# VectorE's ranking halves placed around each dot, and TensorE's background products and queries in halves behind each row's sum

## What is computed

```python
def peer(x, w_q, sub_keys, u_tab, v_tab):
    q = (x @ w_q).reshape(B, S, PEER_HEADS, 2, PEER_HALF)
    scores = jnp.einsum('bshpk,hpnk->bshpn', q, sub_keys)
    s1, i1 = lax.top_k(scores[:, :, :, 0, :], PEER_TOPK)
    s2, i2 = lax.top_k(scores[:, :, :, 1, :], PEER_TOPK)
    cand = (s1[..., :, None] + s2[..., None, :]).reshape(B, S, PEER_HEADS, PEER_TOPK * PEER_TOPK)
    top_s, top_c = lax.top_k(cand, PEER_TOPK)
...
    gates = jax.nn.softmax(top_s, axis=-1).astype(x.dtype)
...
        ue = jnp.take(u_tab, idb, axis=0)
        h = jnp.einsum('thkd,td->thk', ue, xb)
        act = gb * jax.nn.gelu(h, approximate=False)
        ve = jnp.take(v_tab, idb, axis=0)
        return jnp.einsum('thk,thkd->td', act, ve)
```

## Time and profile before

| | |
|---|---|
| median of 3 runs | 1421.67 us (1417.94 to 1422.74) |
| the profiled execution | 1421.98 us, span 1420.3 us |
| mean granted clock of PE | 0.896 of full speed |
| PE, DVE, ACT, POOL busy | 80%, 76%, 66%, 44% of the span |
| read from HBM | 578.60 MB, 409 GB/s over the span |

### The profile page before, as it was taken

The page is one execution under the profiler, slowest core; times in us unless marked ns, Lnnn a source line. Parts: engine busy times, 40 slices in busy tenths (PEclk is TensorE's granted clock), DMA queues, the critical chain, the costliest instruction groups (busy, mean ns, idle before and its releaser), DMA issues.

```text
span 1420.3 us, 19525 instructions
## 1 busy us (share of the span) xinstructions
PE 1130.9 (80%) x6884; PEld 890.8 (63%) x6884; DVE 1078.1 (76%) x2602; ACT 938.8 (66%) x1617; POOL 625.0 (44%) x572
## 2 busy tenths in 40 slices
PE   9999999998789877696756987877667866776566
PEld 4567777676677776666656566765555655555455
DVE  1488877778778887678766668988887788878857
ACT  2245778679877988766645666667666766667563
POOL 1044444344444554444433434444444555444451
PEclk9999999999889999998777988898789988888968
DMA  9899999999999999999999999999999999999994
GB/s 351 311 383 409 422 425 425 426 425 425 402 426 419 424 423 425 425 424 417 431 422 425 426 426 406 426 425 426 426 426 413 404 423 426 426 425 426 425 400 170
DMA packets 94476, 581.98 MB, mean 410 GB/s; under 512 B 10237, under 2 KB 15781, under 8 KB 31914
## 3 DMA queue, kind: packets, MB, share of 16 engines
q0 software_dynamic: 79552, 536.91, 90.5%
q1 hardware_dynamic: 14826, 43.83, 8.0%
HBM read 578.60 MB, written 2.10 MB: 409 GB/s over the span
## 4 chain that ended last, share of the span: by engine, by line
DMA 40%; PE 30%; DVE 15%; ACT 8%; issue 6%; POOL 2%; SPq 0%; DVEq 0%; POOLq 0%; ACTq 0%
DMA arena<-in_uv,ids 39%; PE ps L1269 11%; DVE arena L1914 8%; ACT arena L1536 3%; PE ps L1082 3%; PE ps L948 3%; POOL arena L691 2%; PE ps L1159 2%; PE ps L740 2%; ACT actv L1529 1%; PE ps L757 1%; PE ps L896 1%; PE ps L824 1%; PE ps L821 1%; ACT L1576 1%
## 5 line engine op out<-in xcount | busy, mean ns | idle before, releaser
L691 POOL DMA_INDIRECT arena<-in_uv,ids x556 | 619.9, 1115 | 734.5 <-DVE hid L1914 338.0
L1269 PE MATMUL ps<-ident,arena 128*128 128x128 f32 x4076 | 608.9, 308 | 273.0 <-ACT arena L1536 271.2
L1269 PEld LDWEIGHTS ps<-ident,arena 128*128 128x128 f32 x4076 | 533.3, 159 | 364.6 <-ACT arena L1536 321.4
L1914 DVE CUSTOM_DVE_ANT_1 arena<-arena 128x1024 f32<-128x1024 f32 x384 | 467.7, 1224 | 187.2 <-DMA arena<-in_uv,ids 183.8
L1536 ACT ACTIVATE arena<-arena,actv 128x1024 f32<-128x1024 f32 x511 | 554.2, 1131 | 0.3 <-ACT actv L1529 0.2
L1526 ACT ACTIVATE gel<-hid 128x2 f32<-128x2 f32 (+1 forms) x257 | 52.0, 202 | 356.0 <-DVE hid L1914 353.2
L1914 DVE CUSTOM_DVE_ANT_0 arena<-arena 128x1024 f32<-128x1024 f32 x128 | 155.4, 1223 | 61.1 <-DMA arena<-in_uv,ids 58.5
L1529 ACT ACTIVATE actv<-gel,gates 128x1 f32<-128x1 f32 x511 | 122.9, 287 | 8.4
L948 PE MATMUL ps<-arena 128*128 128x128 f32 x992 | 120.3, 281 | 0.0
L948 PEld LDWEIGHTS ps<-arena 128*128 128x128 f32 x992 | 118.2, 199 | 0.0
L1082 PE MATMUL ps<-arena 128*128 128x384 f32 x192 | 65.9, 486 | 0.0
(11 more groups left out here) (269 smaller groups left out, 1018.1 us busy)
## 6 DMA issues: line engine op xcount, KB each, us to landing
arena<-in_wq SPq DMA_DIRECT2D x9, 1024.0 KB, 10.2
arena<-in_uv,ids POOLq DMA_INDIRECT x556, 3.8
arena<-in_w_out SPq DMA_DIRECT2D x2, 2048.0 KB, 11.3
arena<-in_w_gate SPq DMA_DIRECT2D x1, 4096.0 KB, 17.2
arena<-in_w_out SPq DMA_DIRECT2D x3, 1024.0 KB, 13.1
arena<-in_w_k SPq DMA_DIRECT2D x4, 512.0 KB, 7.9
arena<-in_w_q SPq DMA_DIRECT2D x2, 1024.0 KB, 10.2
arena<-in_w_v SPq DMA_DIRECT2D x2, 1024.0 KB, 10.2
```

What stands on the lines that cost most here:

```text
L691: nc.gpsimd.indirect_dma_start(out=dst, out_offset=None, in_=a["uv"][:, :], in_offset=bass.IndirectOffsetOnAxis(ap=ids[:, u % 4, c:c + 1], ...
L1269: i = mm(ps[:, run_bank(r) + k // 4, (k % 4) * P:(k % 4 + 1) * P], v_row(u, c)[:, k * P:(k + 1) * P], ident[:, :], is_transpose=True, star ...
L1914: v.tensor_tensor_reduce(out=r, in0=r, in1=x1[t], scale=1.0, scalar=0.0, op0=ALU.mult, op1=ALU.add, accum_out=hid[:, i, c:c + 1]).then_inc ...
```

## The change

On DVE each of the five parts of the ranking is split in two. Part 0 stands between the two dots of a group, part 1 behind the second. Unit 0 keeps its old order. The first MAX_INDEX of a key ranking gets a wait for its own end. On PE each product of four blocks is split into two of two blocks: the first behind the odd row of the step, the second behind the next even row. A query is split into its two halves of eight matmuls, one behind row 10 or 11, the other behind the row after. No computation is added or removed, and the order on POOL, ACT and SP is the same.

```diff
@@
-            def query(u):
+            def query(u, half):
                 t, h, b = UNITS[u]
-                pe.wait_ge(wq_in[b], 16 * len(wq_homes[b]) * wq_load(u)[1])
-                pe.wait_ge(score_used, EARLY[u][0] + 2 if u in EARLY else u)
...
+                if half == 0:
+                    pe.wait_ge(wq_in[b], 16 * len(wq_homes[b]) * wq_load(u)[1])
+                    pe.wait_ge(score_used, EARLY[u][0] + 2 if u in EARLY else u)
...
+                if half == 1:
+                    i.then_inc(q_done, 1)
@@
-            def piece_half(p, half):
+            def piece_half(p, half, part):
                 kind, b = PIECES[p]
-                if half == 0 and p >= 2:
+                k0 = 4 * half + 2 * part
+                if k0 == 0 and p >= 2:
                     wait_taken(p - 2)
@@
+            def products(step, part):
+
                 for p in range(NP):
                     for half in range(2):
                         if step == HALF_AT[p][half]:
-                            piece_half(p, half)
+                            piece_half(p, half, part)
+                for t in range(1, NT):
+                    for i in range(1, 5):
+                        if step == out_step(t, f"p{i}"):
+                            out_product(t, i, part)
+                for i in range(NT - 1):
+                    b = TAIL_AT[TAILS[i]]
+                    if step == b + 1 and i == 0 and part == 0:
+                        pe.wait_ge(bias_kept, 2)
+                    if step in (b + 1, b + 2):
+                        k = 4 * (step - b - 1) + 2 * part
+                        gate_product(i, 0, HALF, k, k + 2, 6)
+                    if step in (b + GATE_1, b + GATE_1 + 1):
+                        k = 4 * (step - b - GATE_1) + 2 * part
+                        gate_product(i, HALF, D, k, k + 2, 4)
@@
             for u in range(NU):
                 for c in range(TOPK):
                     combine(u, c)
+                    if c % 2 == 0 and u * TOPK + c:
+                        products((u * TOPK + c) // 2 - 1, 1)
...
-                    if c == query_row(u) and u + 2 < NU and u + 2 not in EARLY:
-                        query(u + 2)
-                    for e in kept_early(u, c):
-                        query(e)
+                    for half in range(2):
+                        if c == query_row(u) + half and u + 2 < NU and u + 2 not in EARLY:
+                            query(u + 2, half)
+                        for e in kept_early(u, c - half):
+                            query(e, half)
                     if c == 12 and u + 2 < NU:
                         key_scores(u + 2)
                     if c % 2:
+                        products(u * NG + c // 2, 0)
                         background(u * NG + c // 2)
@@
-            def rank_keys(u, half):
-                if half == 0:
-                    dve.wait_ge(score_done, u + 1)
+            def rank_keys(u, half, part):
                 s = ps[:, 7, QD + half * NKEY:QD + (half + 1) * NKEY]
-                step(v.max(out=top[:, half, 0:8], in_=s))
-                v.max_index(out=topi[:, half, 0:8], in_max=top[:, half, 0:8], in_values=s)
...
+                if part == 0:
+                    if half == 0:
+                        dve.wait_ge(score_done, u + 1)
+                    step(v.max(out=top[:, half, 0:8], in_=s))
+                    step(v.max_index(out=topi[:, half, 0:8], in_max=top[:, half, 0:8], in_values=s))
@@
+            def rank(u, g, part):
+
+                first = 0 if u else 2
+                if u + 1 < NU:
+                    if g in (first, first + 1):
+                        rank_keys(u + 1, g - first, part)
+                    if g == (first + 2 if u else 3):
+                        rank_sums(u + 1, part)
+                    if g == (first + 3 if u else 4):
+                        rank_rest(u + 1, part)
+                    if g == (first + 4 if u else 5):
+                        rank_ids(u + 1, part)
@@
                 for c in range(g * GRP, (g + 1) * GRP):
+                    if c % 2 and u:
+                        rank(u, g, 0)
                     r = u_row(u, c)
                     dve.wait_ge(rows_in[c % LANDINGS], landed(u * TOPK + c))
```

More of the change, by code:

```diff
@@ L892, in sum_squares, with project_half @@
                 return i
-            def project_half(bank, src, w, j):
-                for c in range(WB):
+            def project_half(bank, src, w, j, part):
+                for c in range(2 * part, 2 * part + 2):
                     i = mm(ps[:, bank, :], src[:, c, :], w[:, c, j * HALF:(j + 1) * HALF],
-                           start=(c == 0), stop=(c == WB - 1))
+                           start=(c == 0), stop=(c == WB - 1), skip_group_check=True)
                 return i
@@ L1211, in background @@
                         out_piece(t, 0)
-                    for i in range(1, 5):
-                        if step == out_step(t, f"p{i}"):
-                            out_piece(t, i)
                     for j in range(2):
@@ L1778, in rank_ids @@
+            def rank_ids(u, part):
                 i = u % 4
```

146 lines of the change are left out of this document (75 added, 71 removed).

## The result

The changed kernel takes 1429.96 us (median of 9 runs, 1425.17 to 1433.05); the kernel before, in its 9 runs beside them, has a median of 1421.67 us. The ratio is 1.0062, 95% interval 1.005 to 1.0073: 8 to 9 us slower. The forecast was no change, 1421.0, with a range that ended at 1426.5.

The account below looks back on a forecast made before the run. The DMA engines were taken as the bound between head and tail. DVE, PE and key scores each added 0; 1421.98 us less 0.7 us from dry stretches gave 1421.3, with the median 0.3 lower 1421.0 us, range 1416.5 to 1426.5.

Parts of the forecast that it names:

- The odd row behind it ends when it did, since the work ahead of it is the same. Gain: 0: PE: halved products let the even row's sum end up to 1.8 us earlier, the odd row's unchanged; gain 0.
- An issue that comes less than about 3 us late costs DMA nothing: Gather queue: 8.86 us from issue to use, less 5.8 us needed, leaves at least 3.1 us to absorb late issues.
- reserve: Gather queue: the time, at least 3.1 us, by which a gather's issue may come late without costing DMA anything.
- Cost between 0 and 10 us, I take 0: DVE waiting for PE's later key scores: a dot at worst 2.4 us late, under 3.1 us, so 0 taken.
- Rival 2: First two dots of a unit: DVE waits there for key scores beyond 3.1 us; 10 us slower, 1431; chance 0.09.
- None is waited for: Adds on DVE and SP's loads: a product's last portion comes about 2.5 us later, but nothing waits for it.
- It is 426 where PE has no idle time: DMA from 200 to 220 us: 426 GB/s though PE has no idle time, so freeing slots sooner gains 0.
- ring: POOL's gathers, four to five under way: gather n may be issued when dot n-5 is done, then queues behind others.
- The wait behind FIND_INDEX8: DVE, key rankings: 60 added waits of 0.12 us, 7 us in all, land in its waiting for DMA; 0 at the end.
- DVE's halves at 0: DVE: split rankings shift dots by up to 1.4 us, inside the 3.1 us the gather queue covers; cost 0.
- Rival 3: PE: idle time in pieces lowers its clock towards 1.2 GHz; 12 us slower, 1433; chance 0.03.
- Rival 1: Four dry DMA stretches: evened-out releases fill them, winning 3.6 to 6.6 us, say 1416; chance 0.14 with other gains.

Follow-up runs that it names:

- dose runs: Kernel before, with whole products moved between the even and odd row of a pair: only the 12 output portions 1.0051, only the 42 other portions 1.0004.
- group 4: Kernel before: unchanged 0.9995; added wait alone 1.0002; products in halves except the output ones 1.0008; 42 input and gate portions whole between the rows 1.0004.
- group 5: Whole change with output products and queries whole, against the kernel before, 1.0039; the same with each ranking whole between the dots, 1.0037.

## Why the prediction was wrong, step by step

**"The odd row behind it ends when it did, since the work ahead of it is the same. Gain: 0": this step failed, and it costs the most.** The work is the same, the idle time is not. A product behind the odd row lies in the time in which PE waits for ACT's next scaling. I had written, of the query, that "part of it moves into idle time", and did not ask what moves out of it. At 475 us 3.60 us of product lay in a gap of 6.5 us; after the change 1.88 did, and 4.62 us of the gap stayed empty. From row 140 to row 176 the changed kernel falls 4.0 us further behind, PE's change alone 4.5 us. The dose runs (1.0051 against 1.0004) show that it is the output products of the attention stage that pay, and not products in general.

**"An issue that comes less than about 3 us late costs DMA nothing": the threshold failed in the early units, but the end hardly paid for it.** It was taken from pieces between 1000 and 1360 us. At 174.72 us a wait of 2.93 us cost some 1.7 us by the rate of that stretch; one of 2.98 us at 931.12 us was followed by 415 GB/s from 940 to 960 us, where it was 427, which is 0.6 us. Below 2.9 us the scale does not stand out from what single executions differ by. And the reserve is not only a number for one row: in units whose rankings follow each other DVE was busy 4.83 and 4.86 of 5 us behind the wait, so the dots of the next rows were late as well and drew on the same reserve. I had counted the lateness of one dot. Nor had I counted that lateness can be won back: by row 140 0.7 us of it were left.

**"Cost between 0 and 10 us, I take 0" (key scores): the wait was sized right; its price at the end is small or open.** MAX8 waited 6 times, 13.1 us in all, 3.0 at most; I had 5 to 20 us, none over 3. Rival 2 was this mechanism. For the wait of unit 2 the dots say 0.7 us. Taking all of them away (keys behind both dots) brought 1.0062 to 1.004, in another comparison, whose intervals only just touch. One of the waits, 2.98 us at 469.96 us, lies just ahead of the second place, and what it does there was not separated.

**"None is waited for" (the adds that read a product): not so for one of them.** DVE waited 1.31 us at 335.68 us for an output product, 2.83 us when its second half came a whole group later. In the whole change this cost nothing that shows (416 GB/s from 320 to 380 us, 412 before).

**"It is 426 where PE has no idle time": true as read, and used wrongly.** The same load placed late starves the ring: in the kernel with the output products between the rows DMA moved 290 GB/s while PE was busy 5.00 of 5.00 us.

**The wait behind FIND_INDEX8: right,** 1.0002 alone. In that run the instruction behind it starts 0.32 us after the start of FIND_INDEX8:

```profile
251.64 0.29 DVE L1745 FIND_INDEX8 topi<-top,ps 128x8 uint32<-128x128 f32 x1
251.96 0.09 DVE L1746 MATCH_VALUE_LOAD left<-top,ps 128x8 f32 x1
```

Before it was 0.20 us (504.65 and 504.85), so a wait costs DVE the 0.12 us of the forecast. The Trainium skill (VectorE: DVE Perf Modes, "The DRAIN you can't avoid") says that such a semaphore costs nothing extra; for this pair of instructions the trace shows 0.12 us, and only the end of the kernel shows nothing.

**DVE's halves at 0: not settled.** Alone they gave 1.0016, with the keys taken out 1.0023, and all of it between the dots 1.0001. I have no mechanism for this order, and differences of this size may not be real. What is ruled out is the added wait, and the lateness of the odd dot as a cost by itself.

**Rival 3, the clock: wrong over the whole** (0.906, where it was 0.896; PE busy 1130.5 us, where it was 1130.9). Rival 1, the fill of the dry stretches: the stall's longest "issue" wait fell only to 5.2 us and nothing was won. The stretch from 1100 to 1120 us moved more (411 GB/s against 387). That from 1340 to 1360 us did too (426 against 385), but its neighbours moved less: from 1320 to 1380 us it is 400 against 410.

**What stays open.** The second place is shown, by the trace and by the runs that move its products, with one trace against it (group 4); it is some 4 us of the loss, and no run puts the output products alone back into the whole change. Open are the 3.6 us that the profiled execution had lost by row 32, in one execution only, and what slows the kernels of group 5, whose attention stage moves 420 and 417 GB/s (422 before) and whose loss at unit 2 came back. The two sides alone sum to 0.45% and the whole is 0.62%, which the intervals allow without any interplay; but groups 4 and 5 show parts that do not add.

## What to carry to other kernels

Before a piece of work is moved or split on an engine that is not full, look for the gap in which it lies now and for what that gap waits: the same work a little later, behind the operand that ended the gap, delays every row in the queue. A reserve has to be read in the stretch where the lateness falls, and spent over all rows that the engine serves late, not over the first. A low rate in one stretch is not yet a loss at the end: follow the start of the same row in both traces, and see whether the distance stays. Parts need not add up, so the whole must be timed too.

## What the runs showed of the hardware

The granted clock fell in the gap, and what came next ran slower, whatever it was. In the kernel before 2.91 us of the gap were idle, and the 32 matmul records of four rows behind it took 5.38 us, where the same 32 took 3.96 us ahead of it (granted clock 0.71 from 480 to 485 us, full speed being 2.4 GHz and the other level 1.2 GHz). In the kernel with the output products between the rows PE idled 6.34 us; the first row behind it took 1.97 us instead of 1.04 and the product's eight records 5.18 us instead of 3.60 (0.76 from 490 to 495 us). In the changed kernel, behind 4.62 us, it was 1.97 us for the row and 2.62 us instead of 1.88 for the half product. So the gap costs 1.4 us of slow work before, 1.7 us after the change and 2.5 us with whole products moved. The emptier gap adds 0.3 and 1.1 us by the clock; the larger part of the delay is the product itself, which now stands in front of a waiting row.

A long wait for data need not cost anything. In the changed kernel

```profile
729.75 1.23 DVE L1960 CUSTOM_DVE_ANT_1 arena<-arena 128x1024 f32<-128x1024 f32 x1 [9.79 <-DMA arena<-in_uv,ids]
...
731.76 0.94 POOL L691 DMA_INDIRECT arena<-in_uv,ids  x1 [11.09 <-DVE hid L1960]
```

while DMA moved 467 and 385 GB/s in the two stretches of 5 us ahead of it: 426 in the mean of both, and the next two dots waited only 0.82 and 0.31 us. I read this as transfers that were served together and ended late together; the order of the packets is not shown. A wait of 11.09 us thus went by without any loss in the rate.
